# Two transformer blocks in one kernel: the second mixer's rotation, softmax jobs, map turning and normalisation rearranged

## What is computed

```python
h = rms_norm_2(x, g_mix)
qa, ka, va, qd, kd, vd = split(h @ w_in)        # 512, 128, 128, 512, 512, 512 columns
qa, ka, qd, kd = (apply_rope(t, cos, sin) for t in (qa, ka, qd, kd))
# x1, x2 = halves of 32;  [x1*c - x2*s, x2*c + x1*s]

# sliding window ("swa"): 8 query heads, 2 key heads of 64, window 128, one sink per head
m = max(max(s), sink);  e = exp(s - m);  p = e / (sum(e) + exp(sink - m))
out_a = p @ va

# differential ("diff"): 4 heads, two causal maps each, values of 128
od = (softmax(q1 @ k1) - lam * softmax(q2 @ k2)) @ vd
out_b = rms_norm(od, g_diff) * (1 - lam_init)

x = x + concat(out_a, out_b) @ w_out
```

## Time and profile before

| What | us |
|---|---|
| Median of three runs | 995.76 |
| The profiled execution, its own time | 995.92 |
| Its span, first to last instruction | 994.0 |
| TensorE busy | 952.2 |
| VectorE busy | 664.2 |
| ScalarE busy | 541.2 |
| Units of w_in_2, 617.2 to 674.0 of the span | 56.8 |
| Jobs, turns and products, 674.0 to 715.0 | 41.0 |
| Units of w_out_2, 715.0 to 737.0 | 22.0 |

### The profile page before, as it was taken

One profiled execution on the slowest core, in us unless ns is written; L12 is line 12 of the kernel. 1 busy time (PEld: TensorE's weight loads), 2 busy tenths in 40 slices (PEclk: granted clock), 3 DMA queues, 4 the chain that ended last, 5 costly groups with the idle time before them and its releaser, 6 DMA issues.

```text
span 994.0 us, 17685 instructions
## 1 busy us (share of the span) xinstructions
PE 952.2 (96%) x6228; PEld 817.2 (82%) x6228; DVE 664.2 (67%) x1101; ACT 541.2 (54%) x980; POOL 30.0 (3%) x59
## 2 busy tenths in 40 slices
PE   6999999989989999999999999998899999999997
PEld 5788888879889877888888887887888888888885
DVE  4776766577786467766667785777457366666665
ACT  6564555477545337555555676546646446554452
POOL 3002000000000001000000000002100000000000
PEclk9999999999999999999999999997999999999999
DMA  7677766545220226766656665552047136665652
GB/s 216 201 220 216 207 186 189 154 128 149 85 66 4 65 87 168 212 186 185 189 185 195 189 182 157 170 169 86 1 117 222 49 123 191 191 201 177 194 186 85
DMA packets 204177, 153.62 MB, mean 155 GB/s; under 512 B 5323, under 2 KB 189872, under 8 KB 204128
## 3 DMA queue, kind: packets, MB, share of 16 engines
q1 hardware_dynamic: 202896, 151.08, 50.9%
q0 software_dynamic: 1232, 1.87, 0.9%
HBM read 151.89 MB, written 1.05 MB: 154 GB/s over the span
## 4 chain that ended last, share of the span: by engine, by line
PE 84%; DVE 7%; ACT 5%; issue 2%; DMA 2%; SPq 0%; DVEq 0%; ACTq 0%
PE ps L472 83%; DVE wlo L1652 2%; ACT whi L1149 1%; DMA raw<-in_w_ckv 1%; DMA raw<-in_ffn_w_gate 1%; DVE XT L1697 1%; ACT XT L1186 0%; DMA raw<-in_w_up 0%; ACT arena L1358 0%; DVE X L1720 0%; ACT arena L1170 0%; DVE arena L1889 0%; PE ps L561 0%; DVE arena L1844 0%; ACT arena L1351 0%
## 5 line engine op out<-in xcount | busy, mean ns | idle before, releaser
L472 PE MATMUL ps<-XT,whi 128*128 128x512 f32 (+1 forms) x1584 | 521.9, 382 | 7.5 <-DVE XT L1697 7.5
L1652 DVE TENSOR_TENSOR wlo<-raw,whi 128x1024 fp32r<-128x1024 f32 x280 | 337.1, 1222 | 107.6 <-ACT whi L1149 86.6
L472 PE MATMUL ps<-XT,wlo 128*128 128x256 f32 x1440 | 404.8, 281 | 0.0
L472 PEld LDWEIGHTS ps<-XT,whi 128*128 128x128 f32 x1584 | 289.9, 189 | 69.7 <-issue 7.6
L1149 ACT ACTIVATE whi<-raw 128x1024 fp32r<-128x1024 f32 x280 | 292.4, 1054 | 53.0 <-PE ps L472 21.1
L472 PEld LDWEIGHTS ps<-XT,wlo 128*128 128x128 f32 x1440 | 273.2, 190 | 3.2
L472 PE MATMUL ps<-whi,H 128*128 128x512 f32 x608 | 177.7, 393 | 2.8 <-issue 2.5
L472 PEld LDWEIGHTS ps<-whi,H 128*128 128x128 f32 x608 | 109.0, 188 | 26.0 <-issue 2.7
L472 PE MATMUL ps<-arena 64*64 64x64 f32 (+6 forms) x1576 | 99.6, 250 | 8.6 <-DVE arena L2185 2.0
L472 PEld LDWEIGHTS ps<-arena 64*64 64x64 f32 (+3 forms) x1576 | 91.1, 153 | 16.6 <-DVE arena L2185 2.9
L472 PE MATMUL ps<-wlo,H 128*128 128x512 f32 x304 | 95.6, 393 | 0.0
(11 more groups left out here) (255 smaller groups left out, 713.6 us busy)
## 6 DMA issues: line engine op xcount, KB each, us to landing
raw<-in_ffn_w_gate SPq DMA_DIRECT2D x44, 512.0 KB, 4.6
raw<-in_ffn_w_up SPq DMA_DIRECT2D x44, 512.0 KB, 3.9
raw<-in_ffn_w_down SPq DMA_DIRECT2D x44, 512.0 KB, 4.7
raw<-in_w_in SPq DMA_DIRECT2D x36, 512.0 KB, 3.9
raw<-in_w_up SPq DMA_DIRECT2D x32, 512.0 KB, 4.0
raw<-in_w_down SPq DMA_DIRECT2D x32, 512.0 KB, 4.6
raw<-in_w_out SPq DMA_DIRECT2D x16, 512.0 KB, 3.5
raw<-in_w_ckv SPq DMA_DIRECT2D x16, 512.0 KB, 4.6
```

Source lines behind the costliest of these rows:

```text
L472: return pe.matmul(o, st, mv, start=start, stop=stop, skip_group_check=True)
L1652: dve.tensor_tensor(wlo[:, n % RING, :], raw[:, n % RAW, :], whi[:, n % RING, :].bitcast(F32), sub).then_inc(lo_ready, 1)
```

## The change

It touches `attention()` alone, in every engine's program, and the tables beside it.

- The order of the `w_in_2` units becomes `COLS2`: the eight q and k columns of the differential heads first, then the five of the sliding window, then the five value columns.
- Each unit is made by `a_unit_summed` into one of three banks. ScalarE writes the copy with 32-row halves swapped, as four copies of 32 partitions x 256 columns from PSUM to other partitions (`SWP`), and VectorE rotates from bank and copy. The thirteen `swap32` matmuls, the eighteen low copies and the eighteen additions go; value columns are copied by VectorE. `KSW` is made by two copies on ScalarE.
- Scores are issued in pairs of jobs, alternating between the two halves of the partitions, between units 7 and 17; maxima, exponents and inverses of the first ten jobs follow inside the unit loop, and three groups are turned there.
- The differential maps are combined on VectorE before turning: `invert_sums` of an odd job multiplies its map by minus lambda over its sum (512 columns) and adds the other map times its inverse. `turn` uses `pe.transpose`, one per block, and GpSimd's diagonal matrices go.
- The mask of a differential job is one operation over 512 columns, with a column of zeros added to the constants.
- The sliding-window product puts positions on partitions: the turned block is stationary and 64 value columns move. VectorE normalises it from PSUM (`OSN`), and TensorE turns it with eight transposes.
- The output units take the differential chunks 4 to 7 first (`OUT2_ROWS`); the last four turns and the sliding-window products stand between them.

```diff
-                    [("prev", P), ("diag", P), ("invc", 4 * PAD), ...
+                    [("prev", P), ("diag", P), ("none", P), ("diag1", P), ("invc", 4 * PAD), ...
+        ORDER = [6, 7, 8, 9, 10, 11, 0, 2, 1, 3, 4, 5]
+        COLS2 = [6, 7, 8, 9, 10, 11, 12, 13, 0, 1, 2, 3, 4, 5, 14, 15, 16, 17]
+        OUT2_ROWS = (4, 5, 6, 7, 0, 1, 2, 3)
+        U_BANKS, TURN_BANKS = (4, 5, 6), (7, 7, 7, 3, 3, 4, 5, 4, 5)
...
 TensorE
-                        a_unit(B_WIN2 + i, 0, PS[Q_BANKS[i % 4]], None if i else "mix2")
-                        mm(PS[6 - 4 * (n_rope % 2)][:, 0:T], con("swap32"), QKV[:, k, :]).then_inc(rope_mm, 1)
+                        if i >= 3:
+                            pe.wait_ge(q_sum, i - 2)
+                        a_unit_summed(B_WIN2 + i, PS[U_BANKS[i % 3]], None if i else "mix2")
+                    if i == 7:
+                        pe.wait_ge(rope_done, 6)
+                        scores(0)
...
+                    if i in (15, 17):
+                        scores(i // 2 - 3)
+                    if i in (12, 14, 16):
+                        turn(i // 2 - 6)
...
+                turn(5)
+                turn(6)
+                output(0, start=True)
+                turn(7)
+                turn(8)
+                output(1)
+                output(2)
...
+                        o = PS[6 + n][:, 64 * h:64 * h + 64]
+                            mm(o, pt(j, m, 0), VT2[:, 0, kv], stop=False)
+                            last = mm(o, pt(j, m, 1), VT2[:, 1, kv], start=False)
...
+                output(3)
...
+                for i in range(4, KC):
+                    output(i)
 ScalarE
+                            for a, b in ((0, 1), (1, 0), (2, 3), (3, 2)):
+                                ins = act.activation(SWP[QUADRANTS[a], n_rope % 2, :],
+                                                     PS[U_BANKS[i % 3]][QUADRANTS[b], 0:T], ACT.Copy)
+                            ins.then_inc(q_swap, 1)
+                    if 9 <= i <= 17:
+                        exponents(i - 9)
+                    if i in (13, 15, 17):
+                        turned((i - 13) // 2)
...
+                act.activation(ODS, ODS, ACT.Sqrt, ...).then_inc(od_std, 1)
+                turned(3)
+                turned(4)
...
+                exponents(10)
+                exponents(11)
+                for k in range(5, 9):
+                    turned(k)
 VectorE
+                        dve.tensor_tensor(RT[:, 0, :], bank[:, 0:T], RC, mul).then_inc(q_sum, 1)
+                        dve.tensor_tensor(RT[:, 1, :], SWP[:, n_rope % 2, :], RSN, mul)...
+                        dve.tensor_tensor(QKV[:, k, :], RT[:, 0, :], RT[:, 1, :], add).then_inc(rope_done, 1)
+                    if i >= 8:
+                        maxima(i - 8)
+                    if i >= 10:
+                        invert_sums(i - 10)
...
+                        dve.tensor_tensor(two, two, spread_out(REC[:, q], nk), mul)...
+                            ins = dve.scalar_tensor_tensor(SC[:, j - 1, ks], SC[:, j - 1, ks], REC[:, r:r + 1],
+                                                           SC[:, j, ks], mul, add)
 GpSimd
-                pool.tensor_tensor(turner(j, 0, m)..., bc(ident, m), each(REC[...]), ALU.mult).then_inc(p_ready, 1)
```

More of the change, by code:

```diff
@@ L2217, in attention @@
-                for k in range(12):
-                    maxima(k)
-                    if k:
-                        invert_sums(k - 1)
-                invert_sums(11)
+                        dve.tensor_scalar(REC[:, q], REC[:, q], NLAM, None, mul).then_inc(own_dve, own.next())
+                        dve.wait_ge(own_dve, own.n)
+                        nk = (n + 1) * P
+                        two = SC[:, j, :].rearrange("p (m k) -> p m k", m=m)
+                        dve.tensor_tensor(two, two, spread_out(REC[:, q], nk), mul).then_inc(own_dve, own.next())
```

405 lines of the change are left out of this document (207 added, 198 removed).

## The result

The changed kernel took 990.41 us (median of four runs, 989.63 to 991.72) beside 995.84 for the kernel before on the same chip (median of four, 995.55 to 997.40): a ratio of 0.9948, interval 0.9936 to 0.9960, or 5.4 us less. The forecast was 985.0, with a range of 982.0 to 990.0. Its profiled execution took 990.36 us with a span of 988.6.

The account below looks back on a forecast made before the run. TensorE was taken to bound the unit loop before, VectorE the changed loop's second half. Loop 66.0, middle 11.4 and output units 31.5 sum to 108.9 against 119.8 us: 995.9 - 10.9 = 985.0, range 982.0 to 990.0.

Parts of the forecast that it names:

- late splits: Rival: output units 6, 7 and first w_cq_2 split late, TensorE may wait at next stage; 1 to 5 us, chance 0.10.
- The loop's first half: w_in_2 loop to the end of unit 8: nine summed units and the first pair of score jobs, 27.1 us.
- Its second half: w_in_2 loop, units 9 to 17: VectorE bounds, and TensorE has turned the last column 38.9 us after unit 8.
- turn 0: Turn behind unit 12 in the loop: TensorE waits about 2.5 us for VectorE's first combined map.
- my bounds of 1.3 to 1.7: ScalarE's four copies per unit in the loop: 1.3 to 1.7 us, taken as 1.3.
- The middle: From the loop to the first output unit: products with values, squares, root, evictions and handovers, 11.4 us.
- my first rival: Clock falls behind the loop, over the first output unit: 1 to 4 us more, 986 to 989, chance 0.25.
- The output units: Eight output units with turns, sliding-window products and transposes between them: 31.5 us in sum.
- turn 7: Turn behind the first output unit: TensorE waits 1.6 us for ScalarE's table load, two jobs and an eviction.
- the added table load: Ahead of the cross attention's root: lies beside eight w_cq_2 units; without that cover it would cost 1.3 us.
- Elsewhere: nothing: Outside the stage: reordered loads and 131 KB more constants cost nothing, at most 0.7 us.
- The rival on the slower side: Clock stays down from the wait behind unit 12, eating the gain; at 26 us the kernel takes 997; chance 0.04.

Follow-up runs that it names:

- one-pass kernel: Changed kernel with VectorE combining two maps in one pass, unnormalised, without the product of 512 columns; 0.9946 of before.
- the filler: Changed kernel with six matmuls without use on constants put between turns 3 and 4, where TensorE waits 3 us; 0.9933 of before.
- spread splits: Combined kernel with the splits of w_out_2 units 4 and 5 and the last early split moved; 0.9895 with an early root, 985.51 us without.
- combined kernel with filler: Changed kernel with early splits, later turns, one-pass combination, turn 3 earlier, chunk transposes between unit halves, and six useless matmuls behind turn 4; 0.9941 of before.
- early splits: Changed kernel splitting output units 6 and 7 and the first of w_cq_2 ahead of the sliding-window chunks; 990.21 us, 0.9947 of before.
- the filler at the cross attention: Kernel with spread splits and early root, plus four matmuls without use between the cross attention's scores and its turns; 0.9883 of before.

## Why the prediction was wrong

Two steps failed: the size of the terms ahead of the first output unit, 2.8 us in both profiles, and late splits, which the sum had at nothing and which cost 1.05 to 2.3 us. A third part, the clock at the cross attention, came in one profile of two.

**The loop's first half** was right: 27.10 of 27.1. **Its second half** took 40.5, not 38.9. VectorE bounds most of it, with turn 0 waiting 2.09 (forecast 2.5); the kernel without the combination and the one-pass kernel both show it. What was mis-sized is the start. ScalarE's timeline:

```profile
642.25 1.54 ACT L1532 ACTIVATE arena<-ps 32x256 f32<-32x256 f32 x4 [1.51 <-PE ps L474]
650.08 1.54 ACT L1532 ACTIVATE arena<-ps 32x256 f32<-32x256 f32 x4 [1.35 <-PE ps L474]
```

Unit 8 ended at 641.84, the copies began 0.41 later and took 1.54, so VectorE began 1.98 behind the unit, where I had 1.35: 0.6 us. I took 1.3 inside my bounds of 1.3 to 1.7 and left out the handover. The rotation took 1.20 from start to start instead of 1.13, five times: 0.4. VectorE also waited once for ScalarE's copies (0.45 at 651.65). ScalarE had itself waited 1.35 for TensorE's unit 10 there (second row), and TensorE 0.76 for VectorE's mask ahead of its scores, so this is a handover round all three engines, which the sum had not; that is the rest but for 0.2.

**The middle** took 12.5, not 11.4. From the first product with the values to ScalarE's table load it took 4.15 us, where 2.6 and 1.0 stood, 0.55 more. The second eviction of a turned group, the transposes of the chunks and the half clock stand one behind the other; the filler shows some 0.6 to be the clock. That was my first rival; it came (clock 0.86 in the middle), but fell before the first output unit rather than in it, and cost less than the 1 to 4 us that I gave it. Turning by transpose did not bring it by itself: through the loop, with three groups turned, the clock was 1.00.

**The output units** took 31.30 from first to last matmul start, and 31.5 was forecast to their end: right, in its parts too. The 24 products took 5.28 (forecast 5.0), turn 7 waited 1.16 (1.6), the chunk's handover 0.77 (1.0). ScalarE's table load took 1.28 without a further pause: it starts at 693.70, and the exponents' first instruction at 694.99. This is the place at which the page "ScalarE: Activation LUTs" of the Trainium skill, section "What ACT_TABLE_LOAD costs", would have had 1.4 more; the trace goes against it here. The sum by that page would have been 986.4, not the 986.5 of the prediction.

**Late splits.** The reason for putting them at nothing failed: "four output units last 11 us, and five splits on two engines need about 6". That counts work, and leaves out what the splits wait for: a raw slot is free, and its next load starts, only when the split ahead is done. ScalarE made none from 702.6 to 715.3, so the loads of w_cq_2 came late, and VectorE's update stood in the queue behind. It cost 1.05 to 2.3 us, the gap, shown by the kernels with early and with spread splits. That is inside the 1 to 5 us of the rival, which had a chance of 0.10. I also looked for the cost at TensorE's next units; it came first at the update, that is at the next norm.

**The w_cq_2 units** took 33.33 and 32.55 against 32.09 and 32.48. That this is the late splits' is not shown, since the combined kernel with filler has early splits and 33.38. The chain to the cross attention's turns names something else, in the first profile:

```profile
735.06 1.28 ACT L1192
...
744.87 4.81 DMA raw<-in_w_co
...
752.05 4.67 DMA raw<-in_w_co
```

It runs through ScalarE's added table load, splits and two loads of the next matrix; before, it ran through TensorE's own units. The stretch follows the two loads: 4.81 and 4.67 us with 33.33, 4.42 and 4.29 with 32.55, 4.13 and 4.23 with 32.23 (early splits), 5.02 and 4.51 with 33.38 (combined with filler). The prediction held that the added table load lies beside TensorE's units at no cost. By the chain it has no slack left when the loads are slow; how much of the up to 1.2 us is its own was not tried.

**"Elsewhere: nothing"** missed the clock at the cross attention, 0 or 1.6 us according to the execution. My sum had no term for it. Why it never came in the two profiles of before, whose TensorE waits 2.54 us at the same place, stays open; the change's variants had it behind waits as short.

In the first profile 2.8 + 0.2 + 5.1 of the 10.9 were lost. The table's second column loses 2.8 + 0.2 + 1.5, and by it the kernel would have stood at 989.5, inside the range. The timed median of 5.4 us gained lies between the two stages' gains, 2.8 and 6.4. In the first profile 2.5 us of the gain come from the earlier start of unit 0, which is luck by the profiles above. The rival on the slower side did not come; its clock falls are there, but under waits.

The versions with spread splits reach what the sum promised: 0.9895 and, with the filler at the cross attention, 0.9883 of before (10.5 and 11.7 us less), against 0.9948 for the change. They keep its design and change the order of some twenty lines, and the one-pass combination. They reach the number by other terms than the forecast's: the first output unit still comes 78.86 after unit 0, not 77.4, and the output units take 28.88 where 31.1 was forecast.

## What to carry to other kernels

When work is put into or taken out of a stage that lives on a stream of splits and loads, write down for each split when its slot becomes free and when its load can start; engine time alone hides the wait. On an in-order engine, never put what the critical path needs (an update, a normalisation) behind an operation that waits for a load, and look again after each gain, since a shorter stage meets the same loads earlier. Moving the update alone gained nothing here, as the splits then stood ahead of the next thing that was needed. Read two profiles of the same program before a difference of 1 to 3 us is given a cause.

## What the runs showed of the hardware

- Matmuls of 64 and 32 moving columns past a full 128x128 fp32 block cost the same at full clock, 0.10 to 0.11 us per record, two records per product.
- The granted clock fell to half, 2.4 to 1.2 GHz, in the middle of the 24 products of 32 columns (0.68 over 712 to 714, 0.50 after), though TensorE was busy the whole time. That is one profile; with 64 columns it did not fall there in fifteen.
- Half-clock stretches of 1.6 us cost come and go between executions of one program; matmuls without use in an idle stretch of about 3 us left none there in the four profiles of kernels that had such a filler, and the gain was 0.3 to 1.6 us, as far as other waits had not covered the fall. One kernel had none in the middle without a filler.
- Four copies of 32 partitions from PSUM to other partitions took 1.54 us, no less each (0.38) than one of 128 partitions and as many columns (0.38 to 0.39).
- Loads of one 512 KB unit stood in the chain for 4.1 to 6.1 us, and between two executions of one program the same load took 6.07 and 4.84.
